# Half of the one-hots' products moved from VectorE to GpSimd in the stage of the first weights

## The chip, the cores and the metric

The kernel runs on one core of a Trainium2 chip. The metric is the device time of one execution in microseconds. The core's engines are named as the profile names them: PE (TensorE, with PEld for its weight loads), DVE (VectorE), ACT (ScalarE), POOL (GpSimd) and SP (SyncE). SBUF is the on-chip memory that all of them read, PSUM the one into which PE writes.

## What is computed

The reference is one layer of a diffusion backbone (attention, retention, then a retrieval over 16384 one-neuron experts). Only the retrieval matters here:

```
def block(xb):                                   # 128 tokens
    q = (xb @ w_pq).reshape(128, 8, 256)
    s1, s2 = scores of the two halves of q against 128 + 128 sub-keys
    v1, i1 = lax.top_k(s1, 16);  v2, i2 = lax.top_k(s2, 16)
    cand = v1[..., :, None] + v2[..., None, :]
    top_s, sel = lax.top_k(cand, 16)             # 8 heads x 16 = 128 pairs (i, j) a token
    g = softmax(top_s)
    act = gelu(u_table[eidx] . xb)               # eidx = i * 128 + j
    return sum over the pairs of g * act * v_table[eidx]
```

There are 1152 tokens in 9 tiles of 128. The kernel computes the retrieval of six of the tiles densely: for each of these tokens it builds a table of weights W[i, j] over all 128 x 128 experts, with the token's shares g at its 128 pairs and zero elsewhere, and then multiplies with the whole u and v tables.

## The kernel before

**Stages.** Modulation, projection, attention, retention and scores come first. `stage_experts` comes last and takes from about 1773 us to the end at 4164 us. It works on the six dense tiles in two groups of 384 tokens (GT), and on the three other tiles by gathering rows.

**A step of the weights.** `WeightSteps` makes the tables of weights, four tokens (B) in a step, so one group has 96 steps (STEPS). The partition is one of a token's 128 pairs. In a step DVE compares the numbers 0 to 127 (`iota`) with the pair's j and with its i, which gives the one-hots `hot_j` (L1747) and `hot_i` (L1748), each 128 partitions x 512 fp16 values. It then multiplies `hot_j` with the share. The share is kept as two fp16 numbers, an upper and a lower half (`keep.parts`, k = 0 and 1), so there are two products `hot_w` (both L1751). PE makes for each of the four tokens the product of `hot_i` and `hot_w`, upper and lower halves accumulated in PSUM, which is eight matmuls of 128x128 (L1760). ACT copies the result of the step from PSUM to `wt` in SBUF (L1768). After every four steps SP stores a block of 16 tokens to memory (`store`, L1775).

**Buffers and waits.** The one-hots and products have two buffers each (s = 0, 1), and in this stage PE has two PSUM banks, `pw` and `p_a`. DVE starts step n when PE has finished step n - 2 (`pw_full`). PE starts step n when DVE's last product is there (`hot_full`) and ACT has read the bank (`pw_read`). ACT starts when PE has finished. In the tables of the profile the operand names of these instructions are those of the memory they lie in: `pairsT` is the iota, `gate` the indices and shares.

**The stage of the first weights.** The steps of the first group run ahead of everything else in the stage (`weight_steps`: two steps written out, then a loop of two steps a turn), from 1779 us to 1929 us. The steps of the second group are made later, one for each of 96 of the 128 experts' blocks j, between other work of DVE, with one bank (`blocks`, `weights=`).

**POOL in that stage.** POOL's queue holds in this order: the load of `h_lo`, six gathers of rows (L1975, after the indices are there), then a wait for all of the first group's stores (`w.stored`), and behind it the loads of `w_ring` (L1967), the first of which all products with the u and v tables wait for. SP, in its first block, starts its stores after two loads of u and v. ACT splits two blocks of u and v and the tokens' columns (L1932, L1937, L1948) ahead of its first step.

Of the kernel before, what the change touches and what calls it, by code (L numbers as in the profile page):

```python
# [11 lines left out]
ALU = mybir.AluOpType  # L12
# [3 lines left out]
P = 128  # L16
# [18 lines left out]
N_KEYS = 128  # L35
# [57 lines left out]
class Links:  # L93


    def __init__(self, eng, sem):
        self.eng, self.sem, self.base, self.n = eng, sem, 0, 0
# [939 lines left out]
def wait_count(eng, sem, count):  # L1037

    if not isinstance(count, int) or count > 0:
        eng.wait_ge(sem, count)  # L1040
# [669 lines left out]
class WeightSteps:  # L1710
# [11 lines left out]
    def __init__(self, nc, sem, m, keep, iota):  # L1722

        B = self.B
        self.nc, self.keep = nc, keep
        self.hot_i = [m.sb(f"hot_i{i}", [P, self.SETS, N_KEYS, self.IN], F16) for i in range(2)]
        self.hot_j = [m.sb(f"hot_j{i}", [P, self.SETS, N_KEYS, self.IN], F16) for i in range(2)]
        self.hot_w = [[m.sb(f"hot_w{i}{k}", [P, self.SETS, N_KEYS, self.IN], F16) for k in range(2)] for i in range(2)]
        self.iota = iota.rearrange("p (k b) -> p k b", b=self.IN)
        self.wt = m.sb("wt", [P, 2, N_KEYS, BLOCK])  # L1730
        self.iota_full, self.equal_full, self.hot_full, self.pw_full, self.pw_read, self.wt_free, self.stored, self.stored_next = (
            sem("weights_" + x) for x in ("iota_full", "equal_full", "hot_full", "pw_full", "pw_read", "wt_free", "stored", "stored_next"))

    def keys(self, dve):

# [4 lines left out]
    def vector(self, dve, n, s):  # L1740
# [10 lines left out]
            last = nc.vector.tensor_tensor(self.hot_w[s][k][:], self.hot_j[s][:], column(keep.parts[:, k]), ALU.mult)  # L1751
        last.then_inc(self.hot_full, 1)

    def tensor(self, pe, n, s, banks):

        pe.wait_ge(self.hot_full, n + 1)
        pe.wait_ge(self.pw_read, n + (self.LEAD + 1 - len(banks)))
        for b in range(self.B):
            for k in range(2):
                last = self.nc.tensor.matmul(banks[s % len(banks)][:, b, :], self.hot_i[s][:, b // self.IN, :, b % self.IN],  # L1760
                                             self.hot_w[s][k][:, b // self.IN, :, b % self.IN], start=k == 0, stop=k == 1)
        last.then_inc(self.pw_full, 1)
# [15 lines left out]
def stage_experts(nc, sem, m, keep, a):  # L1778
# [16 lines left out]
    w = WeightSteps(nc, sem, m, keep, keep.pairsT[:, 2, DENSE_AT:DENSE_AT + N_KEYS * WeightSteps.IN // 2].bitcast(F16))  # L1795
# [31 lines left out]
    def out_rows(t):  # L1827
        return a["out"][0][0] if t == 0 else a["out"][1][0, (t - 1) * P:t * P, :]

    def ranks_after(j):  # L1830

        return min(J, j + 1 + (j >= 4) + (j >= 8))

    def weight_steps(eng, body):
        body(0, 0)
        body(1, 1)
        with eng.Fori(1, w.STEPS // 2) as k:
            for s in range(2):
                body(k * 2 + s, s)
# [45 lines left out]
    with nc.Block() as block:  # L1885

        @block.sync
        def _(sp):
            for s in range(SPARSE):
                sp.dma_start(hs[s], keep.h2_dram[:, :, s * P:(s + 1) * P]).then_inc(cols_in[s], 16)  # L1890

            def load(n, j, s):
                wait_count(sp, ulo_full, n - 1)
                sp.dma_start(u_raw[s][:], a["uT"][j]).then_inc(u_in[s], 16)
                wait_count(sp, vlo_full, n - 1)
                sp.dma_start(v_raw[s][:], a["v"][j]).then_inc(v_in[s], 16)

            for g in range(GROUPS):
                def first():
                    if g == 0:  # L1900
                        w.store(sp, 0, w.stored)
                        with sp.Fori(1, BLOCKS) as b:
                            w.store(sp, b, w.stored)

                blocks(sp, g, load, lambda n, j, s: None, first)
            sp.wait_ge(ulo_full, GROUPS * J)
            sp.wait_ge(vlo_full, GROUPS * J)
            for s in range(SPARSE):
                sp.dma_start(x1_sparse[s], keep.x1_dram[s]).then_inc(xs_in, 16)
            for s in range(SPARSE):  # L1910
                sp.wait_ge(sparse_full, s + 1)
                sp.dma_start(out_rows(s), x1_sparse[s]).then_inc(sparse_out, 16)
            for i in range(GROUP):
                sp.wait_ge(y_full, (GROUPS - 1) * GROUP + i + 1)
                sp.dma_start(out_rows(SPARSE + (GROUPS - 1) * GROUP + i), x1[i][:]).then_inc(y_out[1][i], 16)
            sp.wait_ge(sparse_out, 16 * SPARSE)
            for g in range(GROUPS):
                for i in range(GROUP):
                    sp.wait_ge(y_out[g][i], 16)
# [38 lines left out]
        @block.gpsimd  # L1958
        def _(pool):
            CHUNKS = J // JC  # L1960

            def load_w(g, c):

                n = c + g * CHUNKS
                wait_count(pool, w_in, n * 16)
                wait_count(pool, g_full, (n - 1) * JC + 1)
                pool.dma_start(w_ring[:, n % 2], keep.w_dram[g * TB:(g + 1) * TB, :, c * JC:(c + 1) * JC, :].rearrange("b i j t -> i b j t")).then_inc(w_in, 16)  # L1967

            def gather(g, j):

                n = g * J + j
                for s in range(SPARSE):
                    wait_count(pool, rows_used, (n - SLOTS) * SPARSE + s + 1)
                    at = bass.IndirectOffsetOnAxis(ap=keep.experts[:, s, j:j + 1].bitcast(U32), axis=0)
                    pool.indirect_dma_start(rows[s][n % SLOTS][:], None, (keep.u_rows, v_rows)[g], at).then_inc(rows_in[s][n % SLOTS], 16)  # L1975

            def load_x1(g):
                for i in range(GROUP):
                    wait_count(pool, y_out[0][i], 16 * g)
                    pool.dma_start(x1[i][:], keep.x1_dram[SPARSE + g * GROUP + i]).then_inc(x1_in[i], 16)  # L1980

            pool.dma_start(h_lo[:].bitcast(F32), keep.h2_dram[:, :, DENSE_AT:DENSE_AT + GT]).then_inc(h_in, 16)
            pool.wait_ge(idx_done, 2)
            for g in range(GROUPS):
                for j in range(SLOTS):
                    gather(g, j)
                if g == 0:
                    pool.wait_ge(w.stored, 16 * BLOCKS)
                load_w(g, 0)
                load_w(g, 1)  # L1990
                if g == 0:
                    pool.wait_ge(cols_turned, SPARSE)
                    load_x1(0)
                asked = SLOTS
                for j in range(J):
                    for n in range(asked, min(ranks_after(j) + SLOTS, J)):
                        gather(g, n)
                    asked = max(asked, min(ranks_after(j) + SLOTS, J))
                    if g < GROUPS - 1 and j < w.STEPS and j % w.PER_BLOCK == w.PER_BLOCK - 1:
                        w.store(pool, j // w.PER_BLOCK + BLOCKS, w.stored_next, BLOCKS)  # L2000
                    if j % JC == JC - 1 and j // JC + 2 < CHUNKS:
                        load_w(g, j // JC + 2)
                    if g == 0 and j == w.STEPS + 8:
                        pool.wait_ge(w.stored_next, 16 * BLOCKS)
                        pool.dma_start(h_next, keep.h2_dram[:, :, DENSE_AT + GT:DENSE_AT + 2 * GT]).then_inc(h_in, 16)
                    if g and j == 4:
                        for i in range(GROUP):
                            pool.wait_ge(y_full, i + 1)
                            pool.dma_start(out_rows(SPARSE + i), x1[i][:]).then_inc(y_out[0][i], 16)
                    if g and j == 16:  # L2010
                        load_x1(1)

        @block.vector
        def _(dve):
            def link(ins, n):
# [15 lines left out]
            dve.wait_ge(idx_done, 1)  # L2031
            nc.vector.scalar_tensor_tensor(out=keep.experts.bitcast(U32), in0=tiles(1), scalar=float(N_KEYS), in1=keep.dots,
                                           op0=ALU.mult, op1=ALU.add).then_inc(idx_done, 1)
            weight_steps(dve, lambda n, s: w.vector(dve, n, s))

            def split(n, j, s):
                dve.wait_ge(uhi_full, n + 1)
# [278 lines left out]
```

## Time and profile before

| | us |
|---|---|
| median of 3 runs | 4164.3 |
| lowest, highest | 4162.7, 4176.9 |
| the profiled execution | 4165.7 |
| its span in the profile | 4163.9 |
| PE, DVE, POOL, ACT busy | 3768.1, 2975.2, 1694.1, 1233.2 |

The profile is of one execution. Times in it are counted from the start of the span. The profiled execution is 1.4 us above the median of the runs, less than the runs differ among themselves. A group of instructions is given as line, engine, operation, output<-inputs, shape and count.

### The profile page before, as it was taken

To read this page: it belongs to the slowest core of one execution; us is meant where nothing else is said; L and a number is where in the kernel's file an instruction comes from. 1 tells how busy PE (TensorE), PEld (TensorE's weight loads), DVE (VectorE), ACT (ScalarE), POOL (GpSimd) and SP (SyncE) were. 2 spreads that over 40 slices of the span, in tenths; PEclk is the share of its full clock that TensorE was granted. 3 is DMA by queue.
4 is the path that set the end of the run, shared out by engine and by line. 5 is a ranking of instruction groups with operands and counts; after the bars stand their busy time and mean duration, and the time that the engine had idled before them with its cause. 6 is when DMAs were issued, how large, how long until landed. Compare 5 with 4: busy or idle time off the path is not lost.

```text
span 4163.9 us, 58795 instructions
## 1 busy us (share of the span) xinstructions
PE 3768.1 (90%) x19146; PEld 3041.9 (73%) x19146; DVE 2975.2 (71%) x6026; ACT 1233.2 (30%) x1872; POOL 1694.1 (41%) x1074
## 2 busy tenths in 40 slices
PE   8899866999668999367999999999999999999998
PEld 1699833566555444146888888888988999999997
DVE  0322244333351899988999999998889888888888
ACT  0411033222221222165333333333232232332322
POOL 0222100000230223201655555556557677777774
PEclk9799977899779999656999999999999999999999
DMA  7388700466433101056999999999989999999997
GB/s 250 106 270 289 254 10 20 144 202 205 150 111 102 41 30 35 6 212 229 332 345 342 341 348 336 343 342 354 358 305 368 368 332 346 335 343 342 333 345 255
DMA packets 302319, 1018.03 MB, mean 244 GB/s; under 512 B 30394, under 2 KB 61916, under 8 KB 294932
## 3 DMA queue, kind: packets, MB, share of 16 engines
q1 hardware_dynamic: 154052, 484.32, 34.6%
q0 software_dynamic: 128880, 486.07, 31.9%
q10 hardware_dynamic: 19296, 46.67, 2.9%
q8 instruction: 28, 0.46, 0.0%
q14 instruction: 63, 0.52, 0.0%
HBM read 875.22 MB, written 141.72 MB: 244 GB/s over the span
## 4 chain that ended last, share of the span: by engine, by line
PE 33%; DVE 13%; DMA 6%; issue 5%; POOL 1%; ACT 0%; DVEq 0%; SPq 0%; ACTq 0%; POOLq 0%
PE p_y L2169 16%; PE p_a L2157 5%; PE p_a L2154 5%; PE p_a L2153 5%; DVE rows L2063 5%; DMA rows<-u_rows,pairsT 5%; DVE u_lo L2038 2%; DVE v_lo L2045 2%; DVE hot_w L1751 1%; POOL rows L1975 1%; DVE pairsT L2051 1%; DVE g_hi L2054 1%; DMA rows<-in_v,pairsT 1%; DVE hot_j L1747 0%; DMA w_ring<-weights_spill 0%
## 5 line engine op out<-in xcount | busy, mean ns | idle before, releaser
L1975 POOL DMA_INDIRECT rows<-in_v,pairsT x384 | 743.9, 1937 | 286.6 <-DVE h_rows L2076 191.3
L1975 POOL DMA_INDIRECT rows<-u_rows,pairsT x384 | 593.5, 1546 | 489.1 <-DVE pairsT L2063 416.9
L2153 PE MATMUL p_a<-h_hi,u_hi 128*128 128x384 f32 x2048 | 687.9, 336 | 4.1 <-DVE h_lo L2116 2.5
L2154 PE MATMUL p_a<-h_lo,u_hi 128*128 128x384 f32 x2048 | 691.6, 338 | 0.0
L2169 PE MATMUL p_y<-v_hi,g_hi 128*128 128x512 f32 x1536 | 489.4, 400 | 6.8 <-DVE g_hi L2054 6.3
L1937 ACT ACTIVATE v_hi<-v_raw 128x1024 fp32r<-128x1024 f32 x256 | 272.0, 1063 | 747.9 <-PE p_y L2169 731.0
L2063 DVE CUSTOM_DVE_ANT_0 rows<-rows,h_rows 128x1024 f32<-128x1024 f32 x384 | 451.8, 1221 | 54.4 <-DMA rows<-u_rows,pairsT 52.9
L2169 PE MATMUL p_y<-v_lo,g_hi 128*128 128x512 f32 x1536 | 478.2, 392 | 0.0
L2076 DVE SCALAR_TENSOR_TENSOR h_rows<-rows,pairsT,h_rows 128x1024 f32<-128x1024 f32 x381 | 467.4, 1280 | 14.0 <-DMA rows<-in_v,pairsT 14.0
L2157 PE MATMUL p_a<-h_hi,u_lo 128*128 128x384 f32 x2048 | 399.4, 336 | 18.2 <-DVE u_lo L2038 18.2
L2153 PEld LDWEIGHTS p_a<-h_hi,u_hi 128*128 128x128 f32 x2048 | 385.6, 188 | 15.2 <-issue 4.6
L2154 PEld LDWEIGHTS p_a<-h_lo,u_hi 128*128 128x128 f32 x2048 | 385.5, 188 | 9.8
L2169 PE MATMUL p_y<-v_hi,g_lo 128*128 128x512 f32 x1536 | 390.4, 389 | 0.0
L2157 PEld LDWEIGHTS p_a<-h_hi,u_lo 128*128 128x128 f32 x2048 | 359.0, 188 | 22.2 <-DVE u_lo L2038 22.2
L2169 PEld LDWEIGHTS p_y<-v_lo,g_hi 128*128 128x128 f32 x1536 | 289.6, 189 | 66.4
L2169 PEld LDWEIGHTS p_y<-v_hi,g_lo 128*128 128x128 f32 x1536 | 288.3, 188 | 59.9
L2169 PEld LDWEIGHTS p_y<-v_hi,g_hi 128*128 128x128 f32 x1536 | 280.1, 189 | 53.1 <-DVE g_hi L2054 8.5
L2038 DVE TENSOR_TENSOR u_lo<-u_raw,u_hi 128x1024 fp32r<-128x1024 f32 x256 | 311.9, 1219 | 6.1 <-ACT u_hi L1932 5.9
L2045 DVE TENSOR_TENSOR v_lo<-v_raw,v_hi 128x1024 fp32r<-128x1024 f32 x256 | 312.5, 1221 | 1.0 <-issue 1.0
L1768 ACT ACTIVATE wt<-pw 128x512 f32 (+1 forms) x144 | 156.1, 1084 | 406.5 <-PE pw L1760 402.3
L1932 ACT ACTIVATE u_hi<-u_raw 128x1024 fp32r<-128x1024 f32 x256 | 270.1, 1055 | 4.7 <-DMA u_raw<-in_uT 4.7
L1478 PE MATMUL psc<-wc,hs 128*128 128x512 f32 x576 | 251.6, 596 | 0.0
(302 smaller groups left out, 5639.3 us busy)
## 6 DMA issues: line engine op xcount, KB each, us to landing
u_raw<-in_uT SPq DMA_DIRECT2D x256, 512.0 KB
v_raw<-in_v SPq DMA_DIRECT2D x256, 512.0 KB
w_ring<-weights_spill POOLq DMA_DIRECT2D x32, 1536.0 KB
u_rows<-pairsT ACTq DMA_DIRECT2D x64, 512.0 KB
key_cols<-in_uT SPq DMA_DIRECT2D x64, 512.0 KB, 4.2
u_rows<-key_rows SPq DMA_DIRECT2D x64, 512.0 KB
wada<-in_w_ada SPq DMA_DIRECT2D x12, 2048.0 KB, 7.9
weights_spill<-wt SPq DMA_DIRECT2D x24, 1024.0 KB, 3.9
```

Source lines behind the costliest of these rows:

```text
L1478: last = nc.tensor.matmul(psc[:, 4 * b:4 * b + 4, :], hs[:, k, :], wc[:, k, 4 * b:4 * b + 4, :], start=k == 0, stop=k == KD - 1)
L1932: nc.scalar.activation(u_hi[s][:], u_raw[s][:], ACT.Copy).then_inc(uhi_full, 1)
L1937: nc.scalar.activation(v_hi[s][:], v_raw[s][:], ACT.Copy).then_inc(vhi_full, 1)
L1975: pool.indirect_dma_start(rows[s][n % SLOTS][:], None, (keep.u_rows, v_rows)[g], at).then_inc(rows_in[s][n % SLOTS], 16)
L2038: nc.vector.tensor_sub(u_lo[s][:], u_raw[s][:], u_hi[s][:].bitcast(F32)).then_inc(ulo_full, 1)
L2045: nc.vector.tensor_sub(v_lo[s][:], v_raw[s][:], v_hi[s][:].bitcast(F32)).then_inc(vlo_full, 1)
L2063: nc.vector.tensor_tensor_reduce(out=slot[:], in0=slot[:], in1=keep.h_rows[:, s, :], op0=ALU.mult, op1=ALU.add, scale=1.0, scalar=0.0, acc ...
L2076: nc.vector.scalar_tensor_tensor(out=total, in0=slot[:], scalar=share, in1=total, op0=ALU.mult, op1=ALU.add).then_inc(rows_used, 1)
L2153: nc.tensor.matmul(p_a[:, 0:GT], u_hi[s][:, k, :], h_hi[:, k, :], start=k == 0, stop=False)
L2154: nc.tensor.matmul(p_a[:, 0:GT], u_hi[s][:, k, :], h_lo[:, k, :], start=False, stop=False)
L2157: last = nc.tensor.matmul(p_a[:, 0:GT], u_lo[s][:, k, :], h_hi[:, k, :], start=False, stop=k == KD - 1)
L2169: last = nc.tensor.matmul(p_y[i][:, half, :], part[s][:, i * P:(i + 1) * P], vv[s][:, half * 512:(half + 1) * 512], start=begin, stop=stop)
```

## The change

DVE makes in a step of the first group only three instructions: `hot_j`, `hot_i` and the upper product. The lower product is made by POOL, with the same operands and shapes, in a loop of its own that stands behind the six gathers and ahead of the wait for the stores. POOL waits in each step for `equal_full` (DVE's `hot_j` of this step); PE waits for POOL's `lower_full` beside `hot_full`. The steps of the second group are as they were (`len(banks)` is one there, and DVE runs the old `vector`). Nothing else is changed.

```diff
+    def column(self, x, n):
+        shape = [P, self.SETS, N_KEYS, self.IN]
+        return x[:, bass.ds(n * self.B, self.B)].rearrange("p (c b) -> p c b", b=self.IN).unsqueeze(2).to_broadcast(shape)
+
+    def upper_half(self, dve, n, s):
+        nc, keep = self.nc, self.keep
+        keys = self.iota.unsqueeze(1).to_broadcast([P, self.SETS, N_KEYS, self.IN])
+        dve.wait_ge(self.pw_full, n + 1)
+        nc.vector.tensor_tensor(self.hot_j[s][:], keys, self.column(keep.index[:, 1], n), ALU.is_equal).then_inc(self.equal_full, 1)
+        nc.vector.tensor_tensor(self.hot_i[s][:], keys, self.column(keep.index[:, 0], n), ALU.is_equal)
+        dve.wait_ge(self.equal_full, n + 1)
+        nc.vector.tensor_tensor(self.hot_w[s][0][:], self.hot_j[s][:], self.column(keep.parts[:, 0], n), ALU.mult).then_inc(self.hot_full, 1)
+
+    def lower_half(self, pool, n, s):
+        pool.wait_ge(self.equal_full, n + 1)
+        self.nc.gpsimd.tensor_tensor(self.hot_w[s][1][:], self.hot_j[s][:], self.column(self.keep.parts[:, 1], n), ALU.mult).then_inc(self.lower_full, 1)
+
     def tensor(self, pe, n, s, banks):
         pe.wait_ge(self.hot_full, n + 1)
+        if len(banks) == 2:
+            pe.wait_ge(self.lower_full, n + 1)
...
                 if g == 0:
+                    weight_steps(pool, lambda n, s: w.lower_half(pool, n, s))
                     pool.wait_ge(w.stored, 16 * BLOCKS)
                 load_w(g, 0)
...
-            weight_steps(dve, lambda n, s: w.vector(dve, n, s))
+            weight_steps(dve, lambda n, s: w.upper_half(dve, n, s))
```

The order of DVE's instructions at the start of the stage, before the change (ISA and REGISTER_ALU rows set addresses and loop counts):

```order
L2032 SCALAR_TENSOR_TENSOR pairsT<-p_y,pairsT 128x384
L1747 TENSOR_TENSOR hot_j<-pairsT,gate 128x512
L1748 TENSOR_TENSOR hot_i<-pairsT,gate 128x512
L1751 TENSOR_TENSOR hot_w<-hot_j,gate 128x512 x2
L1747 TENSOR_TENSOR hot_j<-pairsT,gate 128x512
```

And after the change, at the same place of DVE:

```order
L2055 SCALAR_TENSOR_TENSOR pairsT<-p_y,pairsT 128x384
L1764 TENSOR_TENSOR hot_j<-pairsT,gate 128x512
L1765 TENSOR_TENSOR hot_i<-pairsT,gate 128x512
L1767 TENSOR_TENSOR hot_w<-hot_j,gate 128x512
L1764 TENSOR_TENSOR hot_j<-pairsT,gate 128x512
```

One of the two products has left each step, and the next step's `hot_j` stands one place earlier. On POOL, from the load of `h_lo` on, the order before the change:

```order
L1982 DMA h_lo<-h_spill 128x8x384
L1975 DMA rows<-u_rows,pairsT 128x1024 x6
L1967 DMA w_ring<-weights_spill 128x24x128 x2
L1980 DMA x1g<-x_spill 128x1024 x3
L1975 DMA rows<-u_rows,pairsT 128x1024 x12
```

And after it, on POOL:

```order
L2004 DMA h_lo<-h_spill 128x8x384
L1997 DMA rows<-u_rows,pairsT 128x1024 x6
L1772 TENSOR_TENSOR hot_w<-hot_j,gate 128x512 x2
L1859 UNCONDITIONAL_BRANCH
L1859 ISA
L1772 ISA
L1772 TENSOR_TENSOR hot_w<-hot_j,gate 128x512
L1771 REGISTER_ALU
L1772 ISA
L1772 TENSOR_TENSOR hot_w<-hot_j,gate 128x512
L1859 REGISTER_ALU
L1859 COMPARE_AND_BRANCH
```

The two first products and the loop with the other 94 have come between the gathers and the loads of `w_ring`, in a place where POOL only waited.

## Rows read from the trace of the kernel before

**Rows 1.** The page's first part: busy time of each engine, share, instructions.

```profile
PE 3768.1 (90%) x19146; PEld 3041.9 (73%) x19146; DVE 2975.2 (71%) x6026; ACT 1233.2 (30%) x1872; POOL 1694.1 (41%) x1074
```

**Rows 2.** Busy time by stretch: PE, PEld, DVE, ACT, POOL (count), PEclk, DMA share, GB/s.

```profile
1803.00:1925.00 122.00, 93.46 (x724) 69.50 (x722) 121.91 (x364) 95.86 (x91) 0.00 (x0) 0.50 0.46 190
```

**Rows 3.** Chain of waits, in order of time, end of the first weights: start, length, what.

```profile
1787.28 146.47 issue
1933.77 12.97 DMA w_ring<-weights_spill
```

**Rows 4.** Timeline, a steady step: start, length, engine, line, instruction, [idle before <-releaser].

```profile
1862.04 0.43 DVE L1747 TENSOR_TENSOR hot_j<-pairsT,gate 128x512 f16<-128x512 f16 x1
...
1862.18 1.04 PE L1760 MATMUL p_a<-hot_w,hot_i 128*128 128x128 f16 x8 [0.30 <-DVE hot_w L1751]
...
1862.38 0.42 DVE L1748 TENSOR_TENSOR hot_i<-pairsT,gate 128x512 f16<-128x512 f16 x1
1862.71 0.75 DVE L1751 TENSOR_TENSOR hot_w<-hot_j,gate 128x512 f16<-128x512 f16 x2
1863.39 0.42 DVE L1747 TENSOR_TENSOR hot_j<-pairsT,gate 128x512 f16<-128x512 f16 x1
...
1863.53 1.04 PE L1760 MATMUL pw<-hot_w,hot_i 128*128 128x128 f16 x8 [0.31 <-DVE hot_w L1751]
1863.56 1.05 ACT L1768 ACTIVATE wt<-p_a 128x512 f32 x1 [0.21 <-SPq L1773]
```

**Rows 5.** Timeline, the first and the last steps of the steady part.

```profile
1800.40 1.00 ACT L1768 ACTIVATE wt<-pw 128x512 f32<-128x512 f32 x1
...
1801.55 1.01 PE L1760 MATMUL pw<-hot_w,hot_i 128*128 128x128 f16 x8 [10.68 <-ACT wt L1768]
...
1802.73 0.43 DVE L1747 TENSOR_TENSOR hot_j<-pairsT,gate 128x512 f16<-128x512 f16 x1 [9.77 <-PE pw L1760]
...
1925.20 0.42 DVE L1747 TENSOR_TENSOR hot_j<-pairsT,gate 128x512 f16<-128x512 f16 x1
...
1926.68 1.03 PE L1760 MATMUL p_a<-hot_w,hot_i 128*128 128x128 f16 x8 [0.31 <-DVE hot_w L1751]
```

**Rows 6.** Timeline of the retention stage, POOL's and DVE's products side by side, twice.

```profile
1114.03 1.04 POOL L1116 TENSOR_TENSOR qb<-zt,dec 128x512 f32<-128x512 f32 x1
...
1114.54 1.07 DVE L1259 TENSOR_TENSOR kf<-zt,dec 128x512 f32<-128x512 f32 x1
1115.02 1.49 POOL L1116 TENSOR_TENSOR kb<-zt,dec 128x512 f32<-128x512 f32 x1
...
1132.92 1.04 POOL L1116 TENSOR_TENSOR qf<-zt,dec 128x512 f32<-128x512 f32 x1 [8.81 <-DMA zt<-z_spill]
1132.98 1.53 DVE L1259 TENSOR_TENSOR kf<-zt,dec 128x512 f32<-128x512 f32 x1 [2.31 <-DMA zt<-z_spill]
1133.92 1.49 POOL L1116 TENSOR_TENSOR qb<-zt,dec 128x512 f32<-128x512 f32 x1
```

**Rows 7.** One line's durations, min/median/max ns: DVE's product of Rows 6, all nine.

```profile
L1259 DVE TENSOR_TENSOR kf<-zt,dec x9: 692/1530/1578, 1114.5 to 1224.7; 128x512 f32<-128x512 f32 x9
```

**Rows 8.** Timeline of the scores stage, 16-bit products on POOL beside DVE.

```profile
1397.73 2.28 DVE L1645 TENSOR_TENSOR mix<-sel_abf,iota 128x2048 bf16<-128x2048 bf16 x1
1397.96 5.98 POOL L1429 TENSOR_TENSOR mix<-mix,step 128x2048 bf16<-128x2048 bf16 x1 [13.37 <-DVE mix L1645]
...
1403.91 4.06 POOL L1429 TENSOR_TENSOR mix<-mix,idxf 128x2048 bf16<-128x2048 bf16 x1
```

**Rows 9.** One line's durations, min/median/max ns: POOL products of two full operands.

```profile
L1132 POOL TENSOR_TENSOR sg<-sg,zt x9: 1260/1263/1266, 1116.5 to 1227.2; 128x512 f32<-128x512 f32 x9
```

**Rows 10.** Timeline of the scores stage: from a DVE result to POOL's start.

```profile
1267.88 1.22 DVE L1606 TENSOR_TENSOR xn<-po,gate 128x1024 f32<-128x1024 f32 x1 [22.71 <-PE po L1464]
1269.25 2.35 POOL L1417 TENSOR_TENSOR x<-x,xn 128x1024 f32<-128x1024 f32 x1 [18.37 <-DVE xn L1606]
```

More of the change, by code:

```diff
@@ L1730, in __init__ @@
         self.wt = m.sb("wt", [P, 2, N_KEYS, BLOCK])
-        self.iota_full, self.equal_full, self.hot_full, self.pw_full, self.pw_read, self.wt_free, self.stored, self.stored_next = (
-            sem("weights_" + x) for x in ("iota_full", "equal_full", "hot_full", "pw_full", "pw_read", "wt_free", "stored", "stored_next"))
+        self.iota_full, self.equal_full, self.hot_full, self.pw_full, self.pw_read, self.wt_free, self.stored, self.stored_next, self.lower_full = (
+            sem("weights_" + x) for x in ("iota_full", "equal_full", "hot_full", "pw_full", "pw_read", "wt_free", "stored", "stored_next", "lower_full"))
     def keys(self, dve):
```

## The prediction

> **What bounds the kernel now.** I read the page first for which engine is busy: over the whole span it is PE, and POOL is idle for more than half of it [rows 1]. That says nothing on this change, which touches one stretch of 150 us. So the second view is the chain of waits there. POOL has nothing to do from 1787.28 us for 146.47 us, and then the load of the weights begins, behind which all that follows waits [rows 3]. The chain calls this stretch "issue", since POOL's wait for the stores has many releasers; what runs in it are the steps of the first weights. Whatever this stretch gains or loses, the end of the kernel gains or loses, one to one.
>
> The third view is the busy time in the steady part. In 122 us DVE is busy 121.91, ACT 95.86, PE 93.46, POOL not at all, and PE's granted clock is 0.50, the lower of its two levels [rows 2]. The fourth is one step of the timeline [rows 4]: a `hot_j` starts at 1862.04 and the next step's at 1863.39. The four DVE instructions of 0.42 us overlap at their ends, and one starts about 0.335 us after the other. PE takes 1.04 us for its eight matmuls, ACT 1.05 us for its copy. The pitch over the whole steady part is (1925.20 - 1802.73) / 91 = 1.346 us, with 92 steps from the fifth on [rows 5]. That is four times 0.336 us, so DVE's instruction rate sets it.
>
> There is a second limit just as near, and the eye passes over it. With two buffers, DVE's `hot_j` of step n + 2 needs PE's step n. From `hot_j` at 1862.04 to PE's start at 1863.53 are 1.49 us, PE's 1.04 us follow, and from PE's end to a DVE start waiting for it are 1802.73 - (1801.55 + 1.01) = 0.17 us [rows 4, 5]. Together 2.70 us for two steps, 1.35 us a step. Relief on DVE alone would thus find PE's turn-around waiting.
>
> **The change, part by part.**
>
> *What DVE loses.* One instruction of four in each of 96 steps. At 0.335 us that leaves 1.005 us a step. If DVE's rate alone counted, the gain would be 91 x 0.34 = 31 us. It can't be had in full: ACT needs 1.05 us a step and PE 1.04 [rows 4].
>
> *What POOL gets.* One product of 128x512 fp16 a step, second operand a share repeated over the keys. The trace has no fp16 product on POOL. The nearest row is a bf16 one whose second operand is also repeated: 4.06 us for 2048 values, 1.98 ns a value, so 1.02 us for 512 [rows 8]. The f32 products of 512 values with a repeated second operand take 1.04 us [rows 6], and those with two full operands 1.26 [rows 9]. I take 1.04; the 1.26 stays as a dearer case. As an upper end I take the longer bf16 product, 5.98 us for 2048 values, as if all of it were work: 1.50 us for 512 [rows 8]. The lower end would be half of 1.04, if two 16-bit values went at once; the bf16 row speaks against it, since it costs per value what the f32 rows cost.
>
> *Whether both run side by side.* This is the term that decides. Twice in the trace POOL and DVE each have a product whose two inputs both lie in SBUF. At 1132.92 POOL starts one and DVE one 0.06 us later [rows 6]. Of the nine instances of that DVE line the shortest takes 0.69 us, the median 1.53 [rows 7]. So DVE's instruction was held for 0.84 us, to 1132.98 + 0.84 = 1133.82, that is 0.90 us after POOL's start and 0.14 us before POOL's end. POOL's next product starts at 1133.92, while DVE's works, and takes 1.49 instead of 1.04: held for 0.45 us, to 1134.37, again 0.14 us before DVE's end at 1134.51. At 1114 us the same numbers come: DVE's 1.07 us end at 1115.61, which is 0.68 us after 1114.03 + 0.90, and POOL's 1.49 us end 1.04 us after 1115.47 [rows 6]. And in the 16-bit stage, POOL's product that starts 0.23 us behind a DVE product takes 5.98 us, the one without such a neighbour 4.06. The difference, 1.92 us, ends at 1399.88, 0.13 us before DVE's end [rows 8]. So the two take turns: each holds the way to SBUF for its duration less 0.14 us, and who asks second waits for the whole of it. All three DVE instructions that are left in a step have two inputs in SBUF, and so has POOL's.
>
> *The sum of a step.* One hold of POOL, 1.04 - 0.14 = 0.90 us. Three DVE instructions: two at their pitch of 0.335 us, and the last before the hand-over 0.42 - 0.14 = 0.28 us. Together 1.85 us, against 1.346 now, which is 0.504 more. Does something leave gaps in this alternation? POOL is released by `hot_j`'s end; a DVE result reaches POOL in 1269.25 - (1267.88 + 1.22) = 0.15 us [rows 10], so POOL asks 0.57 us after `hot_j`'s start, while `hot_i` works (0.335 to 0.62 us). If its address instructions make it a tenth later, it stands behind the upper product and ahead of the next `hot_j`. Either way somebody is always waiting, and the sum is the same. PE then starts about 2.0 us after `hot_j`'s start and is done at 3.1, before the `hot_j` of two steps on at 3.7: the two buffers no longer bind. What is queued behind the held DVE instruction is the next step's `hot_j`, and PE waits for the held product itself.
>
> *The two ends.* The first steady steps start when ACT has its first copy done, at 1800.40 [rows 5]. POOL comes free from its gathers at 1787.28 [rows 3] and needs some 2 us for the products of the first two steps, so its late start is covered by ACT's own splits. At the end PE starts 1.48 us after the last `hot_j` now (1926.68 - 1925.20 [rows 5]) and about 2.0 after the change, which is 0.5 us once. POOL's wait for the stores comes after its last product, and the stores come later still, so the loads are not held up by POOL. Two waits more on PE and POOL a step are in the terms above.
>
> *Sum.* 91 x 0.504 + 0.5 = 46.4 us. The profiled execution would go from 4165.7 to 4212.1; against the median of the runs, 4164.3, it is 4210.7 us.
>
> *Two rules of the Trainium skill beside the rows.* The rows of the alternation give each hold as the duration less 0.14 us [rows 6, 8]. The Trainium skill (SBUF — State Buffer, section "Who interferes with whom") says that a VectorE instruction with two SBUF inputs and a GpSimd instruction that reads SBUF exclude each other, and that the second is blocked until the first finishes. By whole durations a step would be 0.335 x 2 + 0.42 + 1.04 = 2.13 us, and the kernel would take about 4236 us; the trace agrees with the exclusion and not with its full length. The f32 row of a POOL product is 1.04 us [rows 6]. The Trainium skill (GPSIMD Engine Reference, section 3.1 Elementwise) gives about 2.6 cycles a value at 1.2 GHz, an estimate of 1.11 us for 512 values; the sum by it would be about 53 us instead of 46.
>
> **The rivals.**
>
> *Dearer turns.* The alternation holds, but POOL's product costs more than 1.04 us, since its second operand is read in runs of only two values, or since hand-overs cost something that five of them don't show. At 1.26 us [rows 9] a step is 2.07 us and the kernel 4164.3 + 91 x 0.724 + 0.7 = 4231. At 1.50 us [rows 8] a step is 2.31 and the kernel 4253. For it: no row has this operand. Against it: f32 and bf16 rows with repeated operands agree within 2%.
>
> *Not slower: no turns in this form.* The rows of the alternation are of DVE products that need about one cycle a value: 2.28 us for 2048 values [rows 8], 0.69 for 512 [rows 7]. The ones here do 512 values in a pitch of 0.335 us, another way of working, and might leave POOL's way free. Then the two-buffer limit sets the pace: `hot_j` 0.42, to POOL 0.15, POOL 1.04, to PE 0.07 (as from DVE's end at 1863.46 to PE's start at 1863.53 [rows 4]), PE 1.04, to DVE 0.17, together 2.89 us for two steps, 1.445 a step. That is 9 us more than now, 4173 us; at 1.26 us for POOL, 4183. Even this is no gain, because POOL's product is longer than the two DVE pitches it takes out of the turn-around. It turns into a gain where POOL needs less than about 0.85 us. At 0.52 us, half price, the pitch would be 1.19 and the kernel 4150, still within 0.5%. Against this rival: the exclusion showed whichever of the two came first and for 16-bit and 32-bit values alike, and what the instructions have in common is where their inputs lie.
>
> *Faster by more than 0.5%.* This needs a pitch under 1.346 - 20.8 / 91 = 1.117 us, with ACT's copies at 1.05 us and PE's matmuls at 1.04 already there. It would take a free way, a POOL product under 0.4 us and no slack anywhere.
>
> **How the numbers follow.** Taking turns with POOL at 1.00 to 1.15 us: 0.55, time 4207 to 4221; a little less if a hold is shorter. Dearer turns up to 1.50 us: 0.26, time 4221 to 4253. Beyond that: 0.04. No turns, within 0.5%: 0.13, time 4150 to 4183. Faster by over 0.5%: 0.02. A measurement of this kernel can tell about 0.5%, 21 us, from no change; all cases with turns lie above it. So slower 0.85, same 0.13, faster 0.02. The range takes in both cases with turns, with some room below for shorter holds: 4190 to 4253 us. It leaves out 0.19.
>
> **What the profile after would show.** In the stretch of the first weights the pitch of `hot_j` is 1.85 us and the stretch is 46 us longer; the POOL group of the lower products has 96 instructions of about 1.04 us when nothing holds them, and up to 1.3 us with the hold in it. One DVE instruction of each three, most often the upper product, shows some 1.0 to 1.3 us instead of 0.42, the other two 0.42. PE's busy share of the steady part falls from 0.77 to about 0.56 with the clock still at 0.50, and ACT's from 0.79 to about 0.57. The steps of the second group and everything behind the loads are as before, only later. I am wrong in the main term if all DVE instructions stay at 0.42 us: then the pitch shows which of the loop or POOL's own price sets it. I am wrong on the price alone if DVE's held instruction ends late with POOL's mean above 1.2 us.

## The result and the profile after

| | us |
|---|---|
| before, median | 4166.1 (4162.7 to 4176.9) |
| changed, median | 4213.0 (4211.9 to 4217.1) |
| ratio, 95% interval | 1.011, 1.009 to 1.013 |
| the profiled execution, changed | 4217.1, its span 4215.3 |

The medians show the kernel slower by 46.9 us, and the interval of the ratio lies clear of 1. 46 us had been forecast, with a time of 4211 us. Where the time went shows in the stretch of the first weights. The first view is the timeline of one step, as in [rows 4], with POOL in it:

```profile
1861.08 0.41 DVE L1764 TENSOR_TENSOR hot_j<-pairsT,gate 128x512 f16<-128x512 f16 x1
1861.21 1.03 PE L1782 MATMUL pw<-hot_w,hot_i 128*128 128x128 f16 x8 [0.82 <-DVE hot_w L1767]
1861.41 0.41 DVE L1765 TENSOR_TENSOR hot_i<-pairsT,gate 128x512 f16<-128x512 f16 x1
1861.68 1.05 POOL L1772 TENSOR_TENSOR hot_w<-hot_j,gate 128x512 f16<-128x512 f16 x1 [0.80 <-DVE hot_j L1764]
1861.75 1.25 DVE L1767 TENSOR_TENSOR hot_w<-hot_j,gate 128x512 f16<-128x512 f16 x1
...
1862.66 1.06 ACT L1790 ACTIVATE wt<-pw 128x512 f32 x1 [0.85 <-PE pw L1782]
1862.93 0.41 DVE L1764 TENSOR_TENSOR hot_j<-pairsT,gate 128x512 f16<-128x512 f16 x1
```

POOL's product starts at 1861.68, DVE's upper product 0.07 us behind it, and the latter takes 1.25 us where `hot_j` and `hot_i` take 0.41. The next `hot_j` comes 1.85 us after the first. The durations of all instances (minimum, median, maximum in ns), from the view of each line, say that this is no single case:

```profile
L1767 DVE TENSOR_TENSOR hot_w<-hot_j,gate x96: 418/1256/1268, 1782.7 to 1976.4; 128x512 f16<-128x512 f16 x96
...
L1772 POOL TENSOR_TENSOR hot_w<-hot_j,gate x96: 1040/1049/1053, 1790.0 to 1976.4; 128x512 f16<-128x512 f16 x96
...
L1765 DVE TENSOR_TENSOR hot_i<-pairsT,gate x96: 409/412/419, 1782.4 to 1976.1; 128x512 f16<-128x512 f16 x96
```

The busy times of the steady part, in the order of [rows 2]:

```profile
1810.00:1970.00 160.00, 89.42 (x693) 66.46 (x690) 160.00 (x260) 91.32 (x87) 91.14 (x87) 0.50 0.35 144
```

DVE is busy throughout with fewer instructions a microsecond (260 in 160 us, before 364 in 122 us); much of that "busy" is a held instruction. PE's share has gone from 0.77 to 0.56, ACT's from 0.79 to 0.57, and the clock stayed at 0.50. The first and last `hot_j` of the steady part, from the timeline, as in [rows 5], and the end:

```profile
1807.42 0.42 DVE L1764 TENSOR_TENSOR hot_j<-pairsT,gate 128x512 f16<-128x512 f16 x1 [9.12 <-PE pw L1782]
...
1975.76 0.41 DVE L1764 TENSOR_TENSOR hot_j<-pairsT,gate 128x512 f16<-128x512 f16 x1
...
1977.74 1.03 PE L1782 MATMUL p_a<-hot_w,hot_i 128*128 128x128 f16 x8 [0.81 <-DVE hot_w L1767]
...
1984.74 1.51 POOL L1989 DMA_DIRECT2D w_ring<-weights_spill  x1 [7.34 <-DMA weights_spill<-wt]
```

(1975.76 - 1807.42) / 91 = 1.850 us a step, against 1.346. That is 45.9 us more in the steady part and 0.5 in the last step (1.98 us from `hot_j` to PE, 1.48 before).

The two profiled spans differ by 51.4 us, 5 more. They lie ahead of the steady part, which begins at 1807.42 and not at 1802.73: 2.6 us have gone by before the first `hot_j` of the stage (1782.06, before 1779.42), and 2 more at PE's transposes, which waited for a load of `x1g` (PE's third starts at 1791.51 us, before at 1787.19). The change edits neither place. The profiled execution is the slowest of the four changed ones, 4 us above their median, and the medians' difference of 46.9 us is without these 5 us; why they arose is not shown.

### The profile page after: what moved, and what is told of

It reads as the page before. It is cut to its first block, busy times and chain, and to the rows that moved or that the text cites. A ratio compares the mean times of both kernels' runs of the same rounds, so it can differ in the third digit from the quotient of the medians.

```text
span 4215.3 us, 58984 instructions
## 1 busy us (share of the span) xinstructions
PE 3771.5 (89%) x19146; PEld 3044.1 (72%) x19146; DVE 3021.6 (72%) x5930; ACT 1234.2 (29%) x1872; POOL 1794.5 (43%) x1170
## 4 chain that ended last, share of the span: by engine, by line
PE 32%; DVE 15%; DMA 6%; issue 3%; POOL 1%; DVEq 0%; SPq 0%; ACT 0%; ACTq 0%; POOLq 0%
PE p_y L2192 15%; DVE rows L2086 6%; PE p_a L2180 5%; PE p_a L2177 5%; PE p_a L2176 5%; DMA rows<-u_rows,pairsT 5%; DVE u_lo L2061 2%; DVE v_lo L2068 2%; DVE hot_w L1767 1%; PE pw L1782 1%; DVE hot_w L1751 1%; DVE pairsT L2074 1%; POOL rows L1997 1%; DVE g_hi L2077 1%; DMA rows<-in_v,pairsT 1%
```

## The experiments

All have DVE, POOL, PE and ACT in the same stretch, so the pitch of a step is the number to look at. I give it for each from the first and last `hot_j` between 1820 and 1915 us and their count. The median of the kernel before was 4165 to 4167 us in the same sessions. Its single executions lie between 4161 and 4176 us, so of a run with one execution the time alone says little within 10 us; there the pitch and the rows carry the reading.

**Is it the turns or the chain through POOL?** e3 gives DVE all its work back and lets POOL do a product nobody needs.

```diff
     def lower_half(self, pool, n, s):
+        keys = self.iota.unsqueeze(1).to_broadcast([P, self.SETS, N_KEYS, self.IN])
         pool.wait_ge(self.equal_full, n + 1)
-        self.nc.gpsimd.tensor_tensor(self.hot_w[s][1][:], self.hot_j[s][:], self.column(self.keep.parts[:, 1], n), ALU.mult).then_inc(self.lower_full, 1)
+        wait_count(pool, self.lower_full, n)
+        self.nc.gpsimd.tensor_tensor(self.spare[:], keys, self.column(self.keep.parts[:, 1], n), ALU.mult).then_inc(self.lower_full, 1)
...
-            pe.wait_ge(self.lower_full, n + 1)
...
-            weight_steps(dve, lambda n, s: w.upper_half(dve, n, s))
+            weight_steps(dve, lambda n, s: w.vector(dve, n, s))
```

> DVE makes all four instructions of a step as before the change. POOL makes beside them one product of 128x512 fp16 from tiles that nobody writes in this stage, into a spare tile that nobody reads; it waits for hot_j of the step only to keep the pace, and neither PE nor DVE waits for it. Theory (turns): DVE loses POOL's hold of 0.90 us in each step though nobody waits for POOL: pitch 3 x 0.335 + 0.28 + 0.90 = 2.19 us, one DVE instruction of each four held to 1.26 us, kernel 4164 + 91 x 0.84 = 4241 us. Rival (the loss comes from the chain through POOL, PE waiting for POOL's product): no chain, so the pitch stays at 1.35 us and the kernel at 4164 us, all DVE instructions at 0.42 us.

Measured: 4247.6 us (the profiled execution 4243.7), ratio 1.0197 (1.0180 to 1.0214), pitch (1913.0 - 1821.3) / 42 = 2.18 us. The pitch is the theory's 2.19; the median is 7 us above its 4241. The timeline, one step:

```profile
1861.20 1.05 POOL L1775 TENSOR_TENSOR hot_spare<-pairsT,gate 128x512 f16<-128x512 f16 x1 [1.13 <-DVE hot_j L1748]
1861.27 1.59 DVE L1752 TENSOR_TENSOR hot_w<-hot_j,gate 128x512 f16<-128x512 f16 x2
```

The two products of DVE take 1.59 us together, 0.75 before [rows 4]. Nobody waits for POOL here, and the tiles that POOL and DVE share (key numbers, lower shares) are only read by both. Still DVE loses 0.84 us a step. The chain through POOL is out as a cause. One instruction on POOL costs DVE two and a half of its own.

**What must POOL do to hold DVE?** e1 puts a memset in the place of the product, e2 a copy.

```diff
         pool.wait_ge(self.equal_full, n + 1)
-        self.nc.gpsimd.tensor_tensor(self.hot_w[s][1][:], self.hot_j[s][:], self.column(self.keep.parts[:, 1], n), ALU.mult).then_inc(self.lower_full, 1)
+        pool.sem_inc(self.turned, 1)
+        self.nc.gpsimd.memset(self.hot_w[s][1][:], 0.0).then_inc(self.lower_full, 1)
```

> As the changed kernel, but POOL's product is replaced by a memset of the same 128x512 fp16 tile, which writes and reads nothing; the lower half of the shares is left out of the result. Theory (the two engines take turns at reading SBUF, because both have inputs there): an instruction that reads nothing takes no turn, so all three DVE instructions of a step take 0.42 us, and the pitch falls from 1.85 us to what the two buffers allow, about (0.42 + 0.15 + POOL's time, some 0.6, + 0.07 + 1.04 + 0.17) / 2 = 1.23 us, 1.19 at least; the kernel near 4155 us. Rival A (any POOL instruction excludes DVE's): DVE's upper product is still held, by about POOL's time less 0.14 us, and the pitch is 0.95 + 0.46 = 1.41 us. Rival B (the loss is in the waits and address instructions that the split brought, not in the turns): the pitch falls only by what POOL's instruction is shorter, to about 1.4 us, with all DVE instructions at 0.42 us.

Measured in one run: 4163.4 us, pitch (1913.5 - 1820.7) / 71 = 1.31 us. The durations in that stretch, from the views by line:

```profile
L1767 DVE TENSOR_TENSOR hot_w<-hot_j,gate x73: 414/417/421, 1819.8 to 1914.2; 128x512 f16<-128x512 f16 x73
...
L1773 POOL MEMSET hot_w<- x73: 524/525/528, 1819.7 to 1914.1; 128x512 f16 x73
```

None of 73 upper products is held, though POOL's memset of 0.53 us lies over each. So an instruction that only writes takes no turn, and rival A is out. The pitch settles nothing on rival B: 1.31 lies between the theory's 1.23 and B's 1.4. What speaks against B is e3, where the loss is there without the chain, and e5 below, which has the same 1.31 us with no POOL at all.

```diff
-        self.nc.gpsimd.tensor_tensor(self.hot_w[s][1][:], self.hot_j[s][:], self.column(self.keep.parts[:, 1], n), ALU.mult).then_inc(self.lower_full, 1)
+        pool.sem_inc(self.turned, 1)
+        self.nc.gpsimd.tensor_copy(self.hot_w[s][1][:], self.hot_j[s][:]).then_inc(self.lower_full, 1)
```

> As the changed kernel, but POOL copies hot_j to the lower tile instead of multiplying it (one input in SBUF; the lower product is left out of the result). POOL's f32 copies of 128x512 take 0.61 us in the trace of before. Theory: a POOL instruction with one input in SBUF still takes a turn, so DVE's upper product is held for about 0.61 - 0.14 = 0.47 us; pitch 0.95 + 0.47 = 1.42 us, kernel near 4171 us. Rival A (only two full inputs on POOL exclude): DVE's instructions all at 0.42 us and a pitch of 1.2 to 1.25 us, kernel near 4153. Rival B (a turn costs a fixed 0.9 us whatever POOL does): the pitch stays at 1.85 us.

Measured in one run: 4179.4 us, pitch (1914.6 - 1820.9) / 66 = 1.42 us, as the theory has it. The time is 8 us above its 4171, in a single run; in its trace the steady part begins at 1805.29 us, 2.6 us later than before, and the rest was not followed.

```profile
1861.24 0.64 POOL L1773 COPY hot_w<-hot_j 128x512 f16<-128x512 f16 x1 [0.78 <-DVE hot_j L1764]
1861.34 0.82 DVE L1767 TENSOR_TENSOR hot_w<-hot_j,gate 128x512 f16<-128x512 f16 x1
```

DVE's product was held for 0.82 - 0.42 = 0.40 us, to 1861.74, which is 0.50 us after POOL's start and 0.14 before its end. It is the same 0.14 as in [rows 6, 8]. One input on POOL is enough, and the hold goes with POOL's duration.

**What must DVE do to be held?** e6 lets DVE read the key numbers and the upper shares from PSUM, so each of its instructions has one input left in SBUF. POOL's product is untouched.

```diff
-        keys = self.iota.unsqueeze(1).to_broadcast([P, self.SETS, N_KEYS, self.IN])
+        keys = self.iota_ps.unsqueeze(1).to_broadcast([P, self.SETS, N_KEYS, self.IN])
...
-        ...self.column(keep.parts[:, 0], n), ALU.mult).then_inc(self.hot_full, 1)
+        ...self.column(self.parts_ps, n), ALU.mult).then_inc(self.hot_full, 1)
...
+            w.iota_ps = p_y[1][:, 1, 0:N_KEYS * w.IN].rearrange("p (k b) -> p k b", b=w.IN)
+            w.parts_ps = p_y[0][:, 0, 0:GT]
```

> As the changed kernel, but the key numbers and the upper shares that DVE reads lie in PSUM (f32), so that each of its three instructions has one input in SBUF and one in PSUM; POOL's product is as in the changed kernel. DVE's instructions will be slower of themselves, about 0.69 us at a pitch of 0.6. Theory (the turn is for the second way to SBUF, which DVE needs only with two inputs there): none of DVE's instructions is held, all three alike at 0.6 to 0.7 us, POOL's product at 1.04 us; pitch 3 x 0.6 = 1.8 us. Rival (any DVE instruction excludes any POOL product): one DVE instruction of three at about 1.5 us, pitch 1.8 + 0.9 = 2.7 us, kernel 4285 us.

Measured in one run: 4210.7 us, pitch (1914.3 - 1819.3) / 53 = 1.79 us. The timeline:

```profile
1861.45 1.04 POOL L1772 TENSOR_TENSOR hot_w<-hot_j,gate 128x512 f16<-128x512 f16 x1 [0.76 <-DVE hot_j L1764]
1861.73 0.73 DVE L1767 TENSOR_TENSOR hot_w<-hot_j,p_y 128x512 f16<-128x512 f16 x1
...
1862.32 0.73 DVE L1764 TENSOR_TENSOR hot_j<-p_y,gate 128x512 f16<-128x512 f32 x1
```

DVE's product starts in the middle of POOL's and runs through it in the same 0.73 us as its neighbours; the next one too begins before POOL's end. The cost is DVE's own: 0.6 us a pitch instead of 0.335, so the kernel gains nothing. But the turn is gone. Reading from PSUM also made DVE's instructions slower, but that alone doesn't free them: the f32 product of [rows 6, 7] is as slow, 0.69 us, has both inputs in SBUF and is held. Together with e1 this fits one sentence: POOL's reading of SBUF and DVE's reading of a second operand there take turns. It also fits what the Trainium skill says (SBUF — State Buffer, "Who interferes with whom"), that a GpSimd instruction that only writes, or a VectorE instruction with at most one SBUF input outside the two-port modes, does not contend; the 0.42 us of e1 and the 0.73 us of e6 agree.

**Does the price go with the work, and does the order matter?** e4 gives POOL two of the four tokens; e7 swaps DVE's last two instructions.

```diff
+        nc.vector.tensor_tensor(self.hot_w[s][1][:, 1:2], self.hot_j[s][:, 1:2], self.column(keep.parts[:, 1], n)[:, 1:2], ALU.mult).then_inc(self.hot_full, 1)
...
+        self.nc.gpsimd.tensor_tensor(self.hot_w[s][1][:, 0:1], self.hot_j[s][:, 0:1], self.column(self.keep.parts[:, 1], n)[:, 0:1], ALU.mult).then_inc(self.lower_full, 1)
```

> POOL makes the lower product for two of the four tokens (256 values), DVE the rest of it in a fourth, half-sized instruction. Theory: POOL's product takes about 0.54 us and holds 0.40, DVE's instructions take 3 x 0.335 + 0.20 less 0.05 at the hand-over; pitch 1.55 us, kernel 4164 + 91 x 0.21 = 4183 us. So the price per value is what counts, and half the work on POOL costs less than half of the 46 us. Rival (a hand-over has a large fixed price): the pitch stays above 1.75 us. Rival (no turns): pitch 1.28 us, kernel 4158.

Measured in one run: 4191.5 us, pitch (1915.0 - 1820.7) / 58 = 1.63 us, above the expected 1.55. POOL's instruction, all instances:

```profile
L1773 POOL TENSOR_TENSOR hot_w<-hot_j,gate x59: 621/623/625, 1819.7 to 1913.9; 128x256 f16<-128x256 f16 x59
```

It takes 0.62 us, not 0.54: with 1.05 for 512 values, that is 0.20 us fixed and 1.66 ns a value. I had taken the price as in proportion to the size. With a hold of 0.48 the sum is 0.48 + 0.95 + 0.20 = 1.63, as measured. Half the work on POOL costs 0.28 x 91 = 25 us, more than half of the 46, against my expectation.

```diff
+        dve.wait_ge(self.equal_full, n + 1)
+        nc.vector.tensor_tensor(self.hot_w[s][0][:], self.hot_j[s][:], self.column(keep.parts[:, 0], n), ALU.mult)
+        nc.vector.tensor_tensor(self.hot_i[s][:], keys, self.column(keep.index[:, 0], n), ALU.is_equal).then_inc(self.hot_full, 1)
-        nc.vector.tensor_tensor(self.hot_i[s][:], keys, self.column(keep.index[:, 0], n), ALU.is_equal)
-        dve.wait_ge(self.equal_full, n + 1)
-        nc.vector.tensor_tensor(self.hot_w[s][0][:], self.hot_j[s][:], self.column(keep.parts[:, 0], n), ALU.mult).then_inc(self.hot_full, 1)
```

> As the changed kernel with DVE's order hot_j, upper product, hot_i instead of hot_j, hot_i, upper product. Theory: the sum of a step is one hold of POOL and three DVE instructions whoever stands where, so the pitch stays within 0.1 us of 1.85 (the product must wait for hot_j's end, 0.1 us later than its turn) and the held instruction of DVE is hot_i. Rival (the loss is that the upper product, on which PE waits, is held): with hot_i held instead, or with the product through before POOL starts, the pitch falls below 1.7 us.

Measured in one run: 4240.8 us, pitch (1914.9 - 1821.2) / 45 = 2.08 us. The timeline:

```profile
1860.74 0.41 DVE L1764 TENSOR_TENSOR hot_j<-pairsT,gate 128x512 f16<-128x512 f16 x1
...
1861.29 0.43 DVE L1766 TENSOR_TENSOR hot_w<-hot_j,gate 128x512 f16<-128x512 f16 x1
1861.34 1.28 POOL L1772 TENSOR_TENSOR hot_w<-hot_j,gate 128x512 f16<-128x512 f16 x1 [0.80 <-DVE hot_j L1764]
1861.63 1.26 DVE L1767 TENSOR_TENSOR hot_i<-pairsT,gate 128x512 f16<-128x512 f16 x1
```

It is `hot_i` that is held now, as expected, and the rival's pitch below 1.7 us is out. But the pitch is 0.23 us longer, not within 0.1. The product comes 0.55 us after `hot_j`'s start instead of at its turn, 0.335: it waits for `hot_j`'s last value. In the changed kernel `hot_i` fills these 0.22 us. POOL's product shows 1.28 us instead of 1.05: it started 0.05 us behind the upper product and was itself held for 0.23 us, so turns go both ways. The step adds up as 0.55 + 0.28 + 0.90 + 0.335 = 2.07 us. So the sum of a step does depend on the order, by the gaps.

**What was there to gain?** e5 is the change with a POOL that costs nothing: DVE is simply relieved of the lower product.

```diff
-            weight_steps(dve, lambda n, s: w.vector(dve, n, s))
+            for s in range(2):
+                nc.vector.memset(w.hot_w[s][1][:], 0.0)
+            weight_steps(dve, lambda n, s: w.vector(dve, n, s, 1))
```

> The kernel before with DVE's lower product left out of the steps of the first group (the lower tiles are set to zero once, PE's eight matmuls stay; the lower half of those shares is left out of the result). This is the change with a POOL that costs nothing. Theory (second limit): the pitch is not 3 x 0.335 = 1.0 us but the turn-around of two buffers, (0.335 x 2 + 0.42 + 0.07 + 1.04 + 0.17) / 2 = 1.19 us, so the most that the change could have brought is 91 x 0.16 = 14 us, 4150 us. Rival (DVE's rate alone): pitch 1.06 us, set by ACT's copies, 26 us less, 4138 us.

Measured: 4165.0 us, ratio 0.9991 (0.9981 to 1.0000), pitch (1914.6 - 1820.3) / 72 = 1.31 us. Both theories are wrong: the gain in pitch is worth 91 x 0.036 = 3 us, not 14 or 26, and the medians differ by 1.6 us. The timeline says why:

```profile
1860.03 1.01 PE L1760 MATMUL pw<-hot_w,hot_i 128*128 128x128 f16 x8 [0.73 <-ACT wt L1768]
...
1861.45 1.05 ACT L1768 ACTIVATE wt<-pw 128x512 f32 x1 [0.68 <-PE pw L1760]
...
1862.65 1.01 PE L1760 MATMUL pw<-hot_w,hot_i 128*128 128x128 f16 x8 [0.73 <-ACT wt L1768]
```

PE waits for ACT, and ACT for PE, over the bank `pw`: PE 1.01, then 0.41 until ACT starts, ACT 1.05, then 0.15 until PE starts, together 2.62 us for two steps. It is a third limit beside DVE's rate and the two buffers, and it sets e1's pitch too. e8 takes it away by using four banks (two of `p_y` are free in this stretch) on top of e5; e10 does the same to the kernel before. In both the loop has four steps a turn instead of two, and PE waits for the indices before the steps instead of behind them, since the banks of `p_y` held them.

```diff
-            for s in range(2):
-                body(k * 2 + s, s)
+            for s in range(4):
+                body(k * 4 + s, s)
...
-    two_banks = [pw[:], p_a[:].rearrange("p (b k) -> p b k", b=w.B)]
+    two_banks = [x.rearrange("p (b k) -> p b k", b=w.B) for x in (pw[:].rearrange("p b k -> p (b k)"), p_a[:], p_y[1][:, 1, :], p_y[0][:, 0, :])]
```

> The relieved kernel of e5 (DVE's lower product left out in the first group, the lower half of those shares left out of the result) with four PSUM banks for the steps instead of two, and nothing else. In e5 and e1 a step took 1.31 us though DVE had time over: PE waited for ACT to empty the bank of two steps before, (PE 1.01 + 0.42 until ACT starts + ACT 1.05 + 0.14 until PE starts) / 2 = 1.31. Theory (this bank loop is the limit that the prediction missed): with four banks it is gone, and the pitch is that of the two buffers, 1.19 us; kernel 4166 - 91 x 0.16 = 4152 us. Rival (ACT or something else sets 1.31): the pitch stays at 1.31 and the kernel at 4163.

> The kernel before with four PSUM banks for the first group's steps and nothing else. Theory: DVE's four instructions and the two buffers both give 1.35 us, so more banks alone change nothing: pitch 1.34 to 1.35 us. Rival (the banks are the limit before the change too): pitch below 1.30 us.

e8 measured: 4140.1 us, ratio 0.994 (0.9925 to 0.9955), pitch (1890.9 - 1820.4) / 68 = 1.04 us, better than the 1.19 of its theory. The timeline of PE in e8's first steps:

```profile
1796.63 1.04 PE L1760 MATMUL pw<-hot_w,hot_i 128*128 128x128 f16 x8 [7.55 <-ACT wt L1768]
...
1801.42 1.03 PE L1760 MATMUL pw<-hot_w,hot_i 128*128 128x128 f16 x8 [0.39 <-DVE hot_w L1751]
...
1803.77 2.03 PE L1760 MATMUL p_y<-hot_w,hot_i 128*128 128x128 f16 x16 [0.38 <-DVE hot_w L1751]
```

From the first row to the third are six steps in 7.14 us, 1.19 us each: the theory's number. Then something else happened. Busy times by stretch of e8, and below them one of e5:

```profile
1802.00:1804.00 2.00, 1.62 (x16) 1.19 (x14) 1.68 (x6) 1.37 (x2) 0.00 (x0) 0.50 0.25 102
1804.00:1806.00 2.00, 1.80 (x16) 1.31 (x14) 1.75 (x7) 2.00 (x4) 0.00 (x0) 0.59 0.89 373
1806.00:1810.00 4.00, 2.53 (x32) 1.84 (x32) 4.00 (x13) 3.43 (x5) 0.00 (x0) 1.00 0.58 240
...
1820.00:1840.00 20.00, 12.13 (x154) 8.75 (x152) 20.00 (x60) 17.70 (x20) 0.00 (x0) 1.00 0.60 249
```

```profile
1820.00:1915.00 95.00, 68.29 (x576) 55.69 (x576) 76.34 (x220) 70.33 (x74) 0.00 (x0) 0.50 0.49 201
```

With the bank loop gone PE's granted clock rose from 0.50, its lower level, to 1.00, its upper, and eight matmuls take 0.63 us instead of 1.01. That shortens the turn-around as well, to (1.09 + 0.07 + 0.63 + 0.17) / 2 = 0.98 us, and DVE, busy throughout in the rows from 1806 us on, is the limit: 3 x 0.335 = 1.0 us, measured 1.04. e10, in one run: 4166.2 us, pitch (1913.8 - 1819.8) / 69 = 1.36 us, clock 0.50. The pitch is a little above the expected 1.34 to 1.35; banks alone bring nothing, as the theory says.

**A version that lifts all three.** e9 leaves POOL alone. It has the four banks and four buffers, and DVE makes two instructions of 1024 values a step instead of four of 512, one step ahead with the comparison. Recorded ahead of the run: a pitch of 1.20 us and 4153 us; as the rival, a pitch above 2 us if DVE lost its rate by the longer strides or the four open buffers.

```diff
+    def compare(self, dve, n, s):
+        keys = self.iota.unsqueeze(1).unsqueeze(1).to_broadcast([P, self.SETS, 2, N_KEYS, self.IN])
+        wait_count(dve, self.pw_full, n - 1)
+        self.nc.vector.tensor_tensor(self.hot[s], keys, self.both(self.keep.index, n), ALU.is_equal).then_inc(self.equal_full, 1)
+    def product(self, dve, n, s):
+        dve.wait_ge(self.equal_full, n + 1)
+        self.nc.vector.tensor_tensor(self.hot_w2[s], self.hot_j[s].unsqueeze(2).to_broadcast([P, self.SETS, 2, N_KEYS, self.IN]),
+                                     self.both(self.keep.parts, n), ALU.mult).then_inc(self.hot_full, 1)
...
+            def ahead(n, s):
+                w.compare(dve, n, s)
+                if not (isinstance(n, int) and n == 0):
+                    w.product(dve, n - 1, (s - 1) % 4)
```

> A version without POOL that lifts all three limits. DVE makes both one-hots of a step in one instruction of 1024 values, and both products in another (indices and shares are stored interleaved for it), with the next step's comparison ahead of this step's product; four buffers (two of them in the memory of w_ring, which is free then) and four PSUM banks. An instruction of 1024 values should cost 1024 / 512 x 0.267 + 0.068 = 0.60 us of DVE's rate, so 1.20 us a step against 1.35; turn-around (0.6 x 3 + 0.1 + 0.07 + 1.04 + 0.17) / 4 = 0.8 us does not bind, ACT needs 1.05. Theory: pitch 1.20 us, kernel 4166 - 92 x 0.146 = 4153 us, ratio 0.997. Rival (larger strides or four open buffers cost DVE its rate of two values a cycle): instructions near 1.1 us, pitch above 2 us, kernel slower than 4220.

Measured: 4147.9 us, ratio 0.9957 (0.9943 to 0.9970). The timeline (two of the buffers lie in `w_ring`):

```profile
1820.47 0.68 DVE L1769 TENSOR_TENSOR hot<-pairsT,gate 128x1024 f16<-128x1024 f16 x1
...
1821.07 0.68 DVE L1774 TENSOR_TENSOR w_ring<-w_ring,gate 128x1024 f16<-128x1024 f16 x1
...
1821.67 0.68 DVE L1769 TENSOR_TENSOR hot<-pairsT,gate 128x1024 f16<-128x1024 f16 x1
```

1024 values go at a pitch of 0.60 us, a step in 1.20 us, as forecast, and the rival is out. That is 13 us of the 18; the rest was not taken apart, and what each of the three parts is worth was not separated. It is the fastest of the kernels that compute everything, 65 us below the changed one.

## Why the prediction was right, and where not

**That both engines take turns** was the deciding term, and it held with its size. Read from five hand-overs of the trace before [rows 6 to 8]: a hold is the duration less 0.14 us. After: DVE's product starts at 1861.75 and takes 1.25 instead of 0.42, so it was held to 1862.58, which is 0.90 us after POOL's start, as in [rows 6]. e3, e1, e2 and e6 show cause and conditions.

**POOL's price** was taken as 1.04 us and is 1.05. That choice rested on a bf16 row and f32 rows; it came out right for 512 values only, since the price is not in proportion to the size (e4). That the bf16 row, scaled down in proportion, gave 1.02 us was thus partly luck. The bf16 row of 4.06 us for 2048 lies above 0.20 + 2048 x 0.00166 = 3.6 us, so the line through two points of fp16 doesn't carry over either.

**The sum of a step**, 1.85 us, is what was measured, and so are the last step, 0.5 us, the 0.56 and 0.57 of PE and ACT, and the clock of 0.50.

**"Either way somebody is always waiting, and the sum is the same"** holds for the changed kernel but not for any order of DVE's instructions: e7 opens a gap of 0.22 us a step in which nobody asks.

**The second limit** was there, at 1.35 us, but "the two buffers set the pace" is the step that failed, in the rival without turns. It gave 4150 us for a POOL product of 0.52 us. e1 is that case nearly to the number, with 0.53 us and no turns, and came out at 4163.4 us with a pitch of 1.31, not 1.19. The bank loop had been in sight in [rows 4, 5] (PE 1.04 us, 0.34 to ACT's start, ACT 1.05, 0.15 to PE's start, together 2.58 us for two steps) and was not added up; PE's waits in [rows 4] name DVE alone. It did not touch the forecast, since 1.85 lies above all three limits.

**Slower, with 0.85**, and the range of 4190 to 4253 us hold the result.

## What to carry to other kernels

In this kernel, work moved from DVE to POOL was not taken off DVE, because POOL reads SBUF and DVE has two inputs there: POOL's whole time, less 0.14 us, was added to DVE's (e2, e3, e4 and the change). Look for one DVE instruction in the trace that is longer than its sisters while POOL works; the excess is the hold, and five such rows, with a price for POOL that fitted, gave this kernel's loss within a microsecond of the medians' difference. Before an engine is relieved, add up every loop that returns to it, the PSUM banks' too: here three limits lay at 1.35, 1.35 and 1.31 us. Relieving DVE alone was worth 3 us by the pitch and more banks alone nothing; more buffers alone were not tried.

## What the runs showed of the hardware

The granted clock had not been expected to move. Between 1820 and 1915 us it stood at 0.50, 1.2 GHz, in all kernels but e8 and e9; PE was busy there for 0.47 (e3) to 0.77 of the time (before). In e8 PE was busy for 0.81 of the time in the row from 1802 us and for 0.90 in the next one, in which the clock began to rise; from 1806 us it was at 1.00, 2.4 GHz. In e9 it changed between the two levels, as the mean of a stretch shows:

```profile
1820.00:1840.00 20.00, 17.11 (x136) 12.64 (x133) 20.00 (x34) 17.63 (x18) 0.00 (x0) 0.51 0.53 221
1840.00:1860.00 20.00, 13.78 (x136) 10.21 (x134) 20.00 (x34) 17.58 (x17) 0.00 (x0) 0.75 0.54 224
```

In the first of these rows PE was busy for 0.86 of the time at a mean of 0.51; what makes the clock rise is not shown by these runs. PE's busy time falls in the second row because the same 136 matmuls are faster; the pitch stays at 1.20 us, since DVE sets it. In e8 the same rise took the pitch from 1.19 to 1.04 us, 0.15 us of the 0.27 us that e8's step is shorter than e5's; the other 0.12 are the bank loop.
